# Column tiles for a tail and for routing logits, first-round rows by one-hot products, and an earlier read of the spill count, in a hybrid decoder layer

## The chip, the cores and the metric

One core of a Trainium2 chip runs the whole layer. TensorE (PE), VectorE (DVE), ScalarE (ACT), GpSimd (POOL) and SyncE (SP) each work through a queue of their own and wait for each other by semaphores; SP and POOL also start the transfers (DMA). The metric is the device time of one execution in microseconds, as a median of several. All numbers are float32. The profile comes from one profiled execution.

## The reference, cut to what matters

512 tokens of width 1024, with 16 learned meta tokens in front (L = 528 rows), and one layer:

```
n = rms_norm(h)
u = n @ w_in                     # columns: rwkv r,k,v,wd,ad | sb q,k,v | fox q,k,v | fox forget logit (5) | 3 gates
y_a = rwkv7_time_mix(...)        # 6 heads of 64
y_b = stick_breaking_attention   # 5 heads
y_c = forgetting_attention       # 5 heads
h = h + (g0*(y_a@wp_r) + g1*(y_b@wp_s) + g2*(y_c@wp_f)) @ w_out
t = rms_norm(h)
lg = t @ wg + bg                 # 4 groups;  g_idx = argmax
le = t @ we + be                 # 16 experts, 4 in each group
top 2 experts inside the chosen group, softmax over the two, times p_group
y  = sum_e combine[:, e] * ((silu(t @ w_gate[e]) * (t @ w_up[e])) @ w_down[e])   # hidden width 256
return (h + y)[:, 16:]
```

The values of both attentions are 320 columns wide each, and the forget logit adds 5 columns to the second.

## The kernel before, in words

**Projections.** `qkv_products` (line 1508) is a generator of TensorE steps, one product each. It works through 29 groups of 8 chunks: 20 "q" groups (q and k columns, 128 x 264 products), 8 "v" groups (128 rows by 320 or 325 columns), and one "tail" group: rows 512 to 527 of the values. For these 16 rows it makes two products a chunk, one into PSUM partitions 0 to 15 and one into 32 to 47; each is a step, so the tail has 16. The steps are dealt out by `fill_qkv(n)`. A fixed number of steps goes between the small products of the RWKV recurrence (`META_FILL`, `TURN_FILL`, `LEVEL_FILL` and others, lines 61 to 66); what is left (`HEAD_FILL`, line 331) runs before the recurrence. ScalarE copies each group out (`group_out`, from line 714) at fixed places between its own work. In the recurrence TensorE, ScalarE (`Hm` copy) and VectorE (two masked copies, lines 1113 and 1114) take turns at each of 5 levels in each of three head pairs. `fill_out` counts the copied groups; TensorE waits for all 29 in the last level before it fills with gate products (line 1548).

**Output projection and router.** Tokens lie in four tiles of 128. For each tile TensorE makes two half products with `w_out` (`out_half`, line 1818), VectorE adds the residual (line 1243), TensorE transposes the sum (`second_norm_T`, line 1798), ScalarE and VectorE copy the transposed chunks out (`n2T_low`, `n2T_high`), and `router_logits` (line 1809) makes 8 products with the tile's transposed chunk as the stationary operand and the 20 router columns `rw` as the moving one. Tiles 0 to 2 have their logits behind the second half product of the tile after; tile 3 last. ScalarE takes the norm's scale and writes the normalised rows to `n2`; SP stores them to `n2_rows` in HBM.

**Routing.** From the logits VectorE finds group and experts (lines 1263 to 1289), TensorE ranks the tokens of each expert by products with a triangle and ones (1845, 1847), VectorE compares ranks with 0..127 (`hit`, line 1299) and TensorE turns the hits into tables of token ids and weights for 12 rounds (line 1857). Idle products (`unread`, line 1841) stand where TensorE waits. Each round t holds 96 slots of expert MAIN[t] and 32 of a shared one. POOL gathers the rows of rounds 0, 1, 2 from `n2_rows` by these ids (line 617), later ones as their buffers come free.

**Rounds.** In round t TensorE transposes gathered rows (`rows_T`, line 1861), runs gate and up products on four 32-column tiles (line 1878), transposes the hidden rows (1891) and runs the down products (1904). Expert weights lie in five places and are loaded by SP in the order of `PLAN`; one place (number 4) is the memory of `n2`. Results go back by scattering DMA with add; the last three rounds add to rows gathered from the output and scatter plainly (line 625). At the end POOL, like the other engines, reads the number of spilled expert blocks and passes a loop of 10 turns that does nothing if there are none (lines 660 to 662).

Of the kernel before, what the change touches and what calls it, by code (L numbers as in the profile page):

```python
# [14 lines left out]
ALU = mybir.AluOpType  # L15
ACT = mybir.ActivationFunctionType
# [89 lines left out]
def hybrid_layer(nc, x, meta, g1, w_in, mu, w_up, w0, a_up, a0, k_k, k_a, r_k, ln_g, ln_b, f_b, q_g, k_g,  # L106
# [4 lines left out]
    with ExitStack() as ctx:  # L111
# [35 lines left out]
        rw = sb("rw", [P, DC, NG + NE])  # L147
# [6 lines left out]
        stat = sb("stat", [P, 16])  # L154
        f_min = sb("f_min", [P, 4])
# [164 lines left out]
        STEPS = (NF + 1) * DC  # L320
# [50 lines left out]
        def _(sp):  # L371
# [23 lines left out]
            sp.wait_ge(par, 16)  # L395
            swapped = lambda z, i: z.rearrange("(c h p) -> h p c", h=2, p=HD)[1 - i]
# [88 lines left out]
            sp.wait_ge(sem("lg_psum"), 1)  # L485
            expert_in(4)
            expert_out(4)
            sp.wait_ge(sem("xg_in0"), 16)
# [29 lines left out]
        def _(pool):  # L518
# [115 lines left out]
            for t in range(3):  # L634
                rows_in(t, t)
# [18 lines left out]
            pool.wait_ge(sem("sum_in1"), 32)  # L654
            for t in range(N_SUM, NR):
                pool.wait_ge(sem("y_low"), t + 1)
                pool.wait_ge(sem("y_high"), t + 1)
                final_rows(t, t % 3)
            pool.wait_ge(sem("ov_ready"), 1)
            n_ov = pool.value_load(ovi[0:1, 0:1], min_val=0, max_val=NOV)  # L660
# [16 lines left out]
        def _(act):  # L677
# [36 lines left out]
            def group_out():  # L714
# [19 lines left out]
                else:  # L734
                    done(a.activation(V[0:16, i, 0:SW], ps[0:16, b, 0:SW], ACT.Copy))
                    done(a.activation(V[0:16, i, SW:], ps[32:48, b, 0:SW], ACT.Copy))
                    done(a.activation(flog[0:16, i, :], ps[32:48, b, SW:SW + FH], ACT.Copy), "fill_out")
# [178 lines left out]
            for t in range(NT):  # L916
# [13 lines left out]
                done(a.activation(n2[:, t, :], h[:, t, :], ACT.Copy, scale=rs), "n2_ready")  # L930
# [40 lines left out]
        def _(dve):  # L971
# [4 lines left out]
            done(v.memset(eps_c, EPS), "ms_ready")  # L976
            for j in range(SC):
                done(v.memset(U[:, j, 0:1], 0.0))
# [97 lines left out]
            done(tt(rw[:], rw[:], g2c.rearrange("p (c a) -> p c a", a=1).broadcast_to([P, DC, NG + NE]), ALU.mult))  # L1076
# [171 lines left out]
            for t in range(NT):  # L1248
                residual(t, 0)
                if t >= 1:  # L1250
                    high_chunks_T(t - 1)
                residual(t, 1)
# [9 lines left out]
            lg_ps = ps[:, 2, 0:NT * NGE].rearrange("p (t e) -> p t e", t=NT)  # L1262
# [30 lines left out]
            dve.wait_ge(sem("rank_psum"), 1)  # L1293
            rank_ps = ps[:, 3, 0:NT * NE].rearrange("p (a b) -> p a b", a=1).broadcast_to([P, 2, NT * NE])
# [684 lines left out]
```

## Time and profile before

| | |
|---|---|
| median of 3 runs | 828.03 us (826.21 to 828.31) |
| profiled execution: its own time | 827.06 us |
| its span, first to last instruction | 825.3 us |
| mean granted TensorE clock | 0.994 |
| busy: PE, weight loads, DVE, ACT, POOL | 97%, 56%, 35%, 25%, 12% |
| HBM read, written | 100.32 MB, 10.50 MB (134 GB/s over the span) |

The span is told as busy time of each engine, as the chain of work that ended last, and as DMA traffic. A product of float32 appears as two records (two passes). In rows "x16" is a count of instructions; "[0.61 <-DVE ...]" is idle time of the engine before a row and what ended it.

### The profile page before, as it was taken

Reading aid. Unit: us, or ns where it says so; the run is one execution under the profiler, and the core shown is the slowest. Engines: PE = TensorE matmul, PEld = TensorE weight load, DVE = VectorE, ACT = ScalarE, POOL = GpSimd, SP = SyncE. Lnnn points to the kernel's source line nnn. Section 1 sums busy time; section 2 is a strip of 40 time slices with the busy share of each in tenths; the row PEclk is TensorE's granted clock in tenths of the full one; section 3 lists DMA queues with packets and bytes.
Section 4 is the critical chain, followed back from the end, with each engine's and each line's share of the span. In section 5 each row is a group of like instructions: output and inputs, shape, how many; then the busy total and the mean of one; then the engine's idle time right before and its main releaser. Section 6 shows DMA issues by size and latency. Waiting matters only on the chain.

```text
span 825.3 us, 16795 instructions
## 1 busy us (share of the span) xinstructions
PE 800.2 (97%) x7237; PEld 463.8 (56%) x7237; DVE 287.9 (35%) x542; ACT 202.9 (25%) x406; POOL 102.5 (12%) x214
## 2 busy tenths in 40 slices
PE   9999999999999899899999999999999989999995
PEld 8888888877776554455555555444455533333331
DVE  5334930033333245454444333355211423121122
ACT  4324201122253302334432212710112200111100
POOL 8850000000020100131100000000000011211211
PEclk9999999999999999999999999999999999999998
DMA  7412218100000020536111130754630687999962
GB/s 209 116 51 60 95 52 221 36 3 3 4 4 4 3 53 0 128 71 200 51 52 52 51 77 16 240 172 159 256 152 25 253 318 268 373 382 386 389 252 82
DMA packets 76297, 109.80 MB, mean 133 GB/s; under 512 B 17051, under 2 KB 61227, under 8 KB 72128
## 3 DMA queue, kind: packets, MB, share of 16 engines
q1 hardware_dynamic: 71456, 93.22, 33.6%
q0 software_dynamic: 4768, 15.52, 6.4%
q8 instruction: 57, 0.93, 0.5%
q14 instruction: 16, 0.13, 0.0%
HBM read 100.32 MB, written 10.50 MB: 134 GB/s over the span
## 4 chain that ended last, share of the span: by engine, by line
PE 94%; DVE 3%; DMA 1%; issue 1%; SPq 0%; ACT 0%; POOL 0%; POOLq 0%; DVEq 0%; ACTq 0%
PE ps L1548 21%; PE ps L1878 10%; PE ps L1525 9%; PE ps L1443 9%; PE ps L1824 7%; PE ps L1616 7%; PE ps L1785 5%; PE ps L1904 5%; PE ps L1530 5%; PE ps L1721 2%; PE ps L1768 2%; PE ps L1865 2%; PE ps L1427 1%; PE ps L1752 1%; PE ps L1792 1%; PE ps L1756 1%
## 5 line engine op out<-in xcount | busy, mean ns | idle before, releaser
L1548 PE MATMUL ps<-arena 128*128 128x512 f32 x304 | 141.1, 604 | 0.0
L1548 PEld LDWEIGHTS ps<-arena 128*128 128x128 f32 x304 | 54.2, 189 | 58.9 <-issue 58.1
L1878 PE MATMUL ps<-arena 128*32 128x512 f32 x624 | 86.0, 598 | 0.1
L1443 PE MATMUL ps<-arena 128*128 128x264 f32 x320 | 72.8, 386 | 0.0
L1443 PEld LDWEIGHTS ps<-arena 128*128 128x128 f32 x320 | 60.0, 189 | 11.6 <-ACT arena L758 0.7
L1616 PEld LDWEIGHTS ps<-arena 64*64 64x64 f32 x2784 | 51.5, 134 | 21.9 <-issue 16.2
L1616 PE MATMUL ps<-arena 64*64 64x64 f32 x2784 | 56.9, 220 | 4.3 <-DVE arena L1114 2.4
L1525 PE MATMUL ps<-arena,h 128*128 128x264 f32 x256 | 60.5, 389 | 0.0
L1824 PE MATMUL ps<-arena 128*128 128x512 f32 x128 | 56.2, 594 | 0.0
L1525 PEld LDWEIGHTS ps<-arena,h 128*128 128x128 f32 x256 | 47.5, 189 | 8.6
L1785 PE MATMUL ps<-yT_all,arena 128*128 128x512 f32 x112 | 50.1, 599 | 1.0 <-DMA arena<-in_w_p_fox 1.0
L1878 PEld LDWEIGHTS ps<-arena 128*32 128x32 f32 x624 | 22.9, 109 | 45.1 <-issue 45.1
L1332 DVE TENSOR_TENSOR arena<-ps,chan 128x512 f32<-128x512 f32 x24 | 15.6, 686 | 84.5 <-PE ps L1865 84.4
L1904 PE MATMUL ps<-arena 128*32 128x512 f32 x384 | 43.7, 595 | 0.6 <-DVE arena L1349 0.6
L1530 PE MATMUL ps<-arena 128*128 128x320 f32 (+1 forms) x128 | 40.8, 452 | 0.0
L617 POOL DMA_INDIRECT arena<-n_rows,idx x12 | 11.8, 980 | 231.9 <-DVE idx L1316 224.1
L1824 PEld LDWEIGHTS ps<-arena 128*128 128x128 f32 x128 | 23.7, 189 | 28.2 <-issue 28.2
L1206 DVE COPY arena<-ps 128x128 f32<-128x128 f32 (+3 forms) x20 | 9.8, 491 | 81.9 <-PE ps L1756 81.9
L1548 PE MATMUL ps<-arena,yT_all 128*128 128x512 f32 x80 | 38.0, 607 | 0.0
L1878 PE MATMUL ps<-yT_all,arena 128*32 128x512 f32 x144 | 36.4, 602 | 0.0
L1785 PEld LDWEIGHTS ps<-yT_all,arena 128*128 128x128 f32 x112 | 20.7, 190 | 26.8 <-issue 23.9
L947 ACT ACTIVATE arena<-ps 128x256 f32<-128x256 f32 x12 | 4.6, 385 | 96.3 <-PE ps L1878 96.3
(332 smaller groups left out, 983.9 us busy)
## 6 DMA issues: line engine op xcount, KB each, us to landing
arena<-in_moe_w_down SPq DMA_DIRECT2D x32, 512.0 KB, 13.7
arena<-in_moe_w_gate SPq DMA_DIRECT2D x13, 1024.0 KB, 11.2
arena<-in_moe_w_up SPq DMA_DIRECT2D x13, 1024.0 KB, 16.2
arena<-in_w_in SPq DMA_DIRECT2D x19, 512.0 KB, 3.9
arena<-in_w_in SPq DMA_DIRECT2D x5, 1024.0 KB, 6.0
h<-in_x SPq DMA_DIRECT2D x8, 512.0 KB, 5.6
arena<-in_w_out SPq DMA_DIRECT2D x1, 4096.0 KB, 14.9
h<-in_w_in SPq DMA_DIRECT2D x3, 1024.0 KB, 5.2
```

Of the source, the lines that this page charges most:

```text
L1443: ins = mm(ps[:, 2 * (n % 2) + hf, 0:HALF], w[:, c, j * P:(j + 1) * P], nT[:, c, hf * HALF:(hf + 1) * HALF], start=(c == 0), stop=(c == DC ...
L1525: ins = mm(ps[:, b, 0:HALF], w[:, c, (j % 2) * P:(j % 2 + 1) * P], nT[:, c, k * HALF:(k + 1) * HALF], start=(c == 0), stop=(c == DC - 1))
L1530: ins = mm(ps[0:r, b, 0:nw], nT[:, c, k0:k0 + r], w[:, c, 0:nw], start=(c == 0), stop=(c == DC - 1))
L1548: ins = mm(ps[:, gate_bank(n), :], weights_of_gate(n)[:, c, :], nT[:, c, META:L], start=(c == 0), stop=(c == DC - 1))
L1616: return mm(ps[half(q ^ f_out), bank, c * CH:(c + 1) * CH], lhs(r, c), rhs(r, c), start=start, stop=part != "first", skip_group_check=part ...
L1721: ins = mm(psf[:, o + k0:o + k1], QK[q64, cq, qs], QK[q64, ck, k0:k1], start=True, stop=True)
L1768: ins = mm(o, V[:, k, v0:v0 + HD], pT[:, u % 2, j, k, :], start=(k == 0), stop=False, skip_group_check=True)
L1785: ins = mm(ps[:, bank(b), :], wpr[dc % 2][:, 3 * b + c, :], yT[b][:, c, :], start=(c == 0), stop=(b == 0 and c == 2), skip_group_check=(b ...
L1824: ins = mm(ps[:, out_bank(t, k), :], merged[:, c, t * P:(t + 1) * P], wout[:, c, k * 512:(k + 1) * 512], start=(c == 0), stop=(c == DC - 1))
L1865: ins = tr(ps[:, k, c * P:(c + 1) * P], xg[xs_][:, 4 * k + c:D:DC], ident[:])
L1878: ins = mm(ps[rs, bank, :].rearrange("p (h n) -> p h n", h=2), xgT[:, s, c, rs], w1[ws][:, :, c, :], start=(c == 0), stop=(c == DC - 1))
L1904: ins = mm(ps[rs, 4 + k, :], hT[:, s, c, rs], w2[ws][c][:, 512 * k:512 * k + 512], start=(c == 0), stop=(c == 1))
```

## The change

Four edits, with what they need.

- The tail group becomes 8 steps. Each makes four products, of 160, 160, 160 and 165 columns, into PSUM partitions 0, 32, 64 and 96. `STEPS` is 232 instead of 240, so `HEAD_FILL` is 8 less. ScalarE copies it out in four pieces and the forget logits.
- The router weights are padded with zeros to 32 columns. Logits of tiles 0 to 2 come from one function in the middle of the last half product: the weights are stationary, the tokens move, each tile has 32 output partitions. VectorE copies the 96 x 128 result to SBUF, and TensorE transposes it into the place where all logits are read. Tile 3 is done as before with 32 columns.
- Round 0 no longer gathers. VectorE compares ranks for round 0's two experts at once (`hit_ov`), and TensorE multiplies `n2` by these one-hot columns: the result is the transposed rows. `n2` is written in an order in which each chunk of 128 is contiguous. The weights that go over `n2` are loaded only after this.
- POOL reads the spill count before the last three scatters.

```diff
-        rw = sb("rw", [P, DC, NG + NE])
+        rw_pad = sb("rw", [P, DC, 32])
+        rw = rw_pad[:, :, 0:NG + NE]
-        STEPS = (NF + 1) * DC
+        STEPS = NF * DC
...
             par = sem("g1_in")
             sp.wait_ge(par, 16)
+            sp.wait_ge(sem("rw_clear"), 1)
...
             sp.wait_ge(sem("n2_out"), 16 * NT)
             sp.wait_ge(sem("lg_psum"), 1)
+            expert_out(4)
+            sp.wait_ge(sem("xgT_psum"), 2)
             expert_in(4)
-            expert_out(4)
-            sp.wait_ge(sem("xg_in0"), 16)
+            sp.wait_ge(sem("xg_in1"), 16)
             for t in range(NT):
                 sp.dma_start(out[t * P:(t + 1) * P, :], h[:, t, :]).then_inc(sem("sum_set"), 16)
...
             pool.wait_ge(sem("idx_ready"), 1)
-            for t in range(3):
+            for t in (1, 2):
                 rows_in(t, t)
...
             pool.wait_ge(sem("sum_in1"), 32)
+            pool.wait_ge(sem("ov_ready"), 1)
+            n_ov = pool.value_load(ovi[0:1, 0:1], min_val=0, max_val=NOV)
             for t in range(N_SUM, NR):
                 pool.wait_ge(sem("y_low"), t + 1)
                 pool.wait_ge(sem("y_high"), t + 1)
                 final_rows(t, t % 3)
-            pool.wait_ge(sem("ov_ready"), 1)
-            n_ov = pool.value_load(ovi[0:1, 0:1], min_val=0, max_val=NOV)
...
-                    done(a.activation(V[0:16, i, 0:SW], ps[0:16, b, 0:SW], ACT.Copy))
-                    done(a.activation(V[0:16, i, SW:], ps[32:48, b, 0:SW], ACT.Copy))
-                    done(a.activation(flog[0:16, i, :], ps[32:48, b, SW:SW + FH], ACT.Copy), "fill_out")
+                    for n in range(4):
+                        done(a.activation(V[0:16, i, n * SW // 2:(n + 1) * SW // 2], ps[32 * n:32 * n + 16, b, 0:SW // 2], ACT.Copy))
+                    done(a.activation(flog[0:16, i, :], ps[96:112, b, FW // 2:FW // 2 + FH], ACT.Copy), "fill_out")
...
-                done(a.activation(n2[:, t, :], h[:, t, :], ACT.Copy, scale=rs), "n2_ready")
+                done(a.activation(n2[:, t, :].rearrange("p (c q) -> p c q", c=DC), h[:, t, :].rearrange("p (q c) -> p c q", c=DC), ACT.Copy, scale=rs), "n2_ready")
...
             done(v.memset(eps_c, EPS), "ms_ready")
+            done(v.memset(rw_pad[:], 0.0), "rw_clear")
...
                 if t >= 1:
                     high_chunks_T(t - 1)
+                if t == NT - 1:
+                    dve.wait_ge(sem("lgT_psum"), 1)
+                    done(v.tensor_copy(lgT[0:32 * (NT - 1), :], ps[0:32 * (NT - 1), 3, 0:P]), "lgT_ready")
                 residual(t, 1)
...
             dve.wait_ge(sem("rank_psum"), 1)
+            first_rank = R(0)
+            done(stt(first_rank, ps[:, 3, 0:NT * NE].rearrange("p (t e) -> p t e", t=NT), 1.0, asg, ALU.add, ALU.mult))
+            for e, c0, c1 in ((MAIN[0], 0, CAP), (SHARED[0], CAP, P)):
+                done(tt(hit_ov[:, :, c0:c1], first_rank[:, :, e:e + 1].broadcast_to([P, NT, c1 - c0]), rep(iota_f[:, 1:c1 - c0 + 1], c1 - c0), ALU.is_equal), "first_hit")
...
-                            mm(ps[0:r, b, 0:SW], nT[:, c, k0:k0 + r], slot(i - 1)[:, c, 0:SW], start=(c == 0), stop=(c == DC - 1))
-                            yield
-                            ins = mm(ps[32:32 + r, b, 0:RING_W], nT[:, c, k0:k0 + r], w[:, c, 0:RING_W], start=(c == 0), stop=(c == DC - 1))
+                            for n, (cols, wt) in enumerate(((slice(0, SW // 2), slot(i - 1)), (slice(SW // 2, SW), slot(i - 1)),
+                                                            (slice(0, FW // 2), w), (slice(FW // 2, RING_W), w))):
+                                ins = mm(ps[32 * n:32 * n + r, b, 0:cols.stop - cols.start], nT[:, c, k0:k0 + r], wt[:, c, cols],
+                                         start=(c == 0), stop=(c == DC - 1))
...
-            def router_logits(t):
+            def first_logits():
+                pe.wait_ge(sem("n2T_low"), NT - 1)
+                pe.wait_ge(sem("n2T_high"), NT - 1)
+                for c in range(DC):
+                    for t in range(NT - 1):
+                        ins = mm(ps[32 * t:32 * t + 32, 3, 0:P], rw_pad[:, c, :], n2T[:, c, t * P:(t + 1) * P], start=(c == 0), stop=(c == DC - 1))
+                ins.then_inc(sem("lgT_psum"), 1)
+
+            def last_logits():
...
-                    ins = mm(ps[:, 2, t * (NG + NE):(t + 1) * (NG + NE)], n2T[:, c, t * P:(t + 1) * P], rw[:, c, :], start=(c == 0), stop=(c == DC - 1))
+                    ins = mm(ps[:, 2, 32 * t:32 * t + 32], n2T[:, c, t * P:(t + 1) * P], rw_pad[:, c, :], start=(c == 0), stop=(c == DC - 1))
...
+                    if (t, k, c) == (NT - 1, 1, DC // 2):
+                        first_logits()
                     ins = mm(ps[:, out_bank(t, k), :], merged[:, c, t * P:(t + 1) * P], wout[:, c, k * 512:(k + 1) * 512], start=(c == 0), stop=(c == DC - 1))
...
-                if t >= 1:
-                    router_logits(t - 1)
             second_norm_T(NT - 1, 1)
-            router_logits(NT - 1).then_inc(sem("lg_psum"), 1)
+            pe.wait_ge(sem("lgT_ready"), 1)
+            tr(ps[:, 2, 0:32 * (NT - 1)], lgT[0:32 * (NT - 1), :], ident[0:32 * (NT - 1), 0:32 * (NT - 1)])
+            last_logits().then_inc(sem("lg_psum"), 1)
...
-            unread(3)
+            unread(2)
+            pe.wait_ge(sem("n2T_low"), NT)
+            pe.wait_ge(sem("n2T_high"), NT)
+            pe.wait_ge(sem("n2_ready"), NT)
+            pe.wait_ge(sem("first_hit"), 2)
+
+            def first_rows(k):
+                for c in range(4 * k, 4 * k + 4):
+                    for t in range(NT):
+                        ins = mm(ps[:, k, (c % 4) * P:(c % 4 + 1) * P], n2[:, t, c * P:(c + 1) * P], hit_ov[:, t, :], start=(t == 0), stop=(t == NT - 1))
+                ins.then_inc(sem("xgT_psum"), 1)
+            first_rows(0)
             for j in range(2):
...
-            unread(7)
+            first_rows(1)
+            unread(1)
...
-                        ins = tr(ps[:, k, c * P:(c + 1) * P], xg[xs_][:, 4 * k + c:D:DC], ident[:])
+                        ins = tr(ps[:, k, c * P:(c + 1) * P], xg[xs_][:, (4 * k + c) * P:(4 * k + c + 1) * P], ident[:])
...
-            rows_T(0, 0, 0, 16)
```

Left out are the counts of landed gathers, which follow from the gather that is gone, and the two readings of padded logits.

## Rows read from the trace of the kernel before

**Rows 1.** Page, part 4: shares of the chain that ended last, by engine.
```profile
PE 94%; DVE 3%; DMA 1%; issue 1%; SPq 0%; ACT 0%; POOL 0%; POOLq 0%; DVEq 0%; ACTq 0%
```

**Rows 2.** Chain that ended last, 120 to 284 us: start, us, what.
```profile
119.85 39.42 PE ps L1525 x177
...
215.66 2.92 PE ps L1530 x10
...
256.67 1.84 PE ps L1530 x6
...
259.17 1.09 PE ps L1616 x64
...
261.35 1.14 PE ps L1616 x64
...
264.24 1.16 PE ps L1616 x64
...
282.48 1.94 PE ps L1548 x4
```

**Rows 3.** Waits, 100 to 270 us: engine, line, releaser: total us, times, longest.
```profile
DVE arena L1086 <- PE ps L1575: 39.2, 1, 39.2
```

**Rows 4.** Chain that ended last, 600 to 648 us.
```profile
609.66 1.70 PE ps L1815 x16
...
642.48 0.44 PE ps L1806 x4
...
645.94 1.08 PE ps L1815 x8
```

**Rows 5.** Timeline, 642 to 646 us: start, us, engine, line, operation, [idle before].
```profile
642.58 0.69 DVE L1243 TENSOR_TENSOR h<-h,ps 128x512 f32<-128x512 f32 x1 [6.18 <-PE ps L1824]
...
644.46 0.63 PE L1806 MATMUL ps<-ident,h 128*128 128x128 f32 x4
...
645.20 0.69 DVE L1247 COPY arena<-ps 128x512 f32<-128x512 f32 x1 [1.93 <-PE ps L1806]
```

**Rows 6.** Chain that ended last, 653 to 808 us.
```profile
653.70 0.30 DVE arena L1295
...
655.07 0.70 DVE arena L1299
...
657.12 1.96 PE ps L1857 x16
...
661.38 5.97 DMA arena<-n_rows,idx
...
669.11 8.22 PE ps L1878 x60
...
800.55 7.01 PE ps L1878 x64
```

**Rows 7.** Windows: us, busy of PE, PEld, DVE, ACT, POOL, clock, DMA share, GB/s.
```profile
668.00:671.50 3.50, 3.39 (x18) 1.28 (x20) 1.38 (x2) 0.00 (x0) 0.94 (x1) 0.51 1.02 410
```

**Rows 8.** Timeline of ScalarE, 278 to 283 us.
```profile
281.29 0.43 ACT L735 ACTIVATE arena<-ps 16x320 f32<-16x320 f32 x1
...
282.21 0.17 ACT L737 ACTIVATE arena<-ps 16x5 f32<-16x5 f32 x1
```

**Rows 9.** Window of line 1427 (128-column products) alone: us, PE, PEld, clock, DMA.
```profile
12.90:14.80 1.90, 1.90 (x18) 1.90 (x18) 1.00 0.36 61
```

**Rows 10.** DMA issues at 743.4 to 744 us: count, median us to landing.
```profile
arena<-n_rows,idx POOLq DMA_INDIRECT x1, 13.4
```

**Rows 11.** Line 1815 (logits): ns minimum, median, maximum, first and last start.
```profile
L1815 PEld LDWEIGHTS ps<-rw,arena x64: 186/192/192, 609.1 to 646.7; 128*128 128x128 f32 x64
```

**Rows 12.** Lines 660, 661 and 111 in POOL's queue, 810 to 826 us.
```profile
L660 POOLq TENSOR_LOAD <-ovi x1: 509/509/509, 817.1 to 817.1; - x1
L661 POOLq MOVE  x11: 29/29/38, 817.9 to 822.0; - x11
...
L111 POOLq DRAIN  x1: 2688/2688/2688, 822.4 to 822.4; - x1
```

More of the change, by code:

```diff
@@ L154, in hybrid_layer @@
         stat = sb("stat", [P, 16])
+        lgT = sb("lgT", [P, P])
         f_min = sb("f_min", [P, 4])
@@ L1075, in _ @@
             dve.wait_ge(sem("g1_in"), PARAMS_B)
-            done(tt(rw[:], rw[:], g2c.rearrange("p (c a) -> p c a", a=1).broadcast_to([P, DC, NG + NE]), ALU.mult))
+            done(tt(rw, rw, g2c.rearrange("p (c a) -> p c a", a=1).broadcast_to([P, DC, NG + NE]), ALU.mult))
             dve.wait_ge(sem("consts_ready"), 2)
@@ L1261, in _ @@
             dve.wait_ge(sem("lg_psum"), 1)
-            lg_ps = ps[:, 2, 0:NT * NGE].rearrange("p (t e) -> p t e", t=NT)
+            lg_ps = ps[:, 2, 0:NT * 32].rearrange("p (t e) -> p t e", t=NT)[:, :, 0:NGE]
             done(tt(lgx, lg_ps, row3(stat2[:, 2 * NT:3 * NT], NGE), ALU.mult))
@@ L1807, in second_norm_T @@
                 ins.then_inc(sem("n2T_psum"), 1)
-            def router_logits(t):
+            def first_logits():
[6 more added lines that the diff above has]
+            def last_logits():
+                t = NT - 1
                 for c in range(DC):
@@ L1913, in down_ov @@
                     ins.then_inc(sem("down_low" if k == 0 else "down_psum"), 1)
-            pe.wait_ge(sem("n2T_low"), NT)
-            pe.wait_ge(sem("n2T_high"), NT)
-            rows_T(0, 0, 0, 16)
             for t in range(NR + 1):
@@ L1930, in _ @@
                     pe.wait_ge(sem("xgT_ready"), 2 * t + 2)
-                    rows_T(t + 1, (t + 1) % 2, (t + 1) % 3, 16 * ((t + 1) // 3 + 1))
+                    rows_T(t + 1, (t + 1) % 2, (t + 1) % 3, 16 * ((t + 1) // 3 + ((t + 1) % 3 > 0)))
                 if t >= 1:
@@ L1947, in _ @@
                     ins.then_inc(sem("slots_psum"), 1)
-                    rows_T(t, 0, 0, k * 16 + 16 * (NR // 3 + 1))
+                    rows_T(t, 0, 0, k * 16 + 16 * (NR // 3))
                     gate_up_ov(t, k * 32 + 32 * (SLOT0_LOADS + 1))
```

## The prediction

> **What bounds the kernel now.** First the shares of the chain that ended last [rows 1]: 94% of the span is TensorE. So a microsecond counts only where TensorE issues it or waits for it. I then went to the places where the change touches TensorE's order: the projection stage, the output projection with the router, the start of the expert stage, and the end. In the projection stage TensorE runs products of the q, k, v columns one after the other [rows 2], while VectorE has nothing to do for 39.2 us [rows 3]: there each product saved is time saved. From 215 us on the same products are fillers between the small products of the recurrence [rows 2]. At 256 us a filler of three v products lasts 1.84 us; when the fillers become the short tail products, TensorE stands until VectorE is ready: the recurrence's products end at 261.35 + 1.14 = 262.49 and go on at 264.24, 1.75 us later. There a filler under 1.75 us is free. The router [rows 4, 5] is a chain on TensorE with one hop over VectorE; the routing [rows 6] is a chain over both; then comes 5.97 us of a row gather for which TensorE waits, and a first round (8.22 us) that is 1.2 us longer than a later one (7.01 us), since the granted clock is 0.51 over its first 3.5 us [rows 7]: 1.2 instead of 2.4 GHz, after TensorE had run out of work during that gather.
>
> **Tail values on four column tiles.** The last group was 16 filler steps (two products of 320 and 325 columns for each of 8 chunks); now it is 8 steps of four products of 160 to 165 columns. The fillers in the recurrence keep their number of steps, so the 8 steps come out of the projection stage before them, and every group slides 8 places later.
> - Projection stage: 8 products of 2 passes fewer, 39.42 / 177 = 0.223 us a pass [rows 2]: -3.6. VectorE's wait of 39.2 us [rows 3] says that what follows is ready earlier; I take all of it.
> - Filler places that turn from v to q: a v pass costs (2.92 - 1.84) / 4 = 0.27, a q pass 0.22. Two steps (4 passes) lie where nothing else is waited for: -0.2. The others lie in fillers that VectorE's 1.75 us bounds.
> - The filler before the third head pair: now five v steps like the one at 215.66 (2.92), before 259.17 - 256.67 = 2.50: +0.4.
> - Two fillers of three tail steps become three v steps: 1.84 for 1.75, together +0.2. Three tail steps of four tiles each are under 1.75 us: nothing, VectorE's two masked copies hide them. If that cover were gone they'd cost 3 x 0.27 + 0.22 = 1.0.
> - ScalarE takes the group out in four copies instead of two, then the 5-column one. 320 columns are 0.43 us, 5 are 0.17 [rows 8]; by the line between them 160 are 0.30. Four are 4 x 0.33 = 1.3 with the gaps, two were 2 x 0.46 = 0.9: +0.4. TensorE's next product starts at 282.48 [rows 2], 0.1 us behind the 5-column copy's end: it waited for it, so the 0.4 is on the path.
> Sum -2.8 (bounds: -1 if the sliding opens a wait in each level, -3.8 if the added ones hide).
>
> **Three tiles' logits side by side.** Removed: two calls of 1.70 us [rows 4], and the third, 1.70 us. Added in the middle of the last output product: 8 chunks of three 32-column tiles, 128 moving columns each. No row has this shape; the nearest is the warm-up product of 128 columns, 1.90 / 18 = 0.106 us a pass [rows 9], so 16 passes are 1.7 us if the tiles run beside each other; above, 5.1 us if they don't. I take 1.7: the expert products with their four 32-column tiles do 64 records in 7.01 us [rows 6], that is four tiles in the time of one. To this two changes of tile shape: a filler of 6 passes takes 1.84 where 6 x 0.27 = 1.62, so 0.2 each, 0.4. The last output product has the third call behind it, so up to its end (642.48 before) the path is 3.4 shorter and 2.1 longer: -1.3. Its waits (the transposed rows of tile 2) were asked for an output product earlier; the copy of the logits by VectorE lies before the last residual sum, which waits for TensorE anyway: nothing.
> Behind 642.48: the residual sum ends at 642.58 + 0.69 = 643.27, and the last four transposes, at 644.46 before because the third call stood ahead of them, can start at 643.3 [rows 5]: 1.1 earlier. The copy to n2T (645.20) and the last four logits products (645.94, 1.08) follow them. The transpose of the 96 logits rows and the first four products (0.1 + 0.9) fit into the 0.7 + 0.7 that this hop takes. -1.1. Sum -2.4 (bounds +1 to -3).
>
> **First rows by one-hot products.** Before: routing, gather, transposes, round one. Now, on the times of the trace before: the rank products end at 653.6 [rows 6].
> - VectorE gets three operations ahead of its chain: 64, 384 and 128 elements a partition. 128 are 0.30, 512 are 0.70, so 0.3 + 0.57 + 0.3 = 1.2. The slot values, for which the slot products waited until 657.1, come at 658.3.
> - TensorE: two idle products (4 passes of 512 columns, 7.01 / 16 = 0.44 each) to 655.3; VectorE's hits are there at 653.7 + 1.2 = 654.9. Then 16 products, 32 passes of 128 columns at 0.106: 3.4, to 658.7. The slot products (16 passes, 1.7) to 660.4, for which nothing is waited now. Second 16 products, to 663.8. One idle product, to 664.7. The scaled rows: VectorE has the first half after the slot tables and a copy of the ranks (about 663.4), the second 0.7 (its price for 512 elements) behind 663.8, and round one needs it half a round later. Round one starts at 664.8 instead of 669.1: -4.3.
> - The gather's 5.97 us and the stretch without work in it are gone, and I expect the clock to stay: round one at 7.01 instead of 8.22, -1.2. If it fell all the same, this is the loss.
> - Next late: rows of round two. POOL now asks for them first. The gather was issued 2.3 us behind the slot products (661.38 for 659.08), now at 662.95, landing at 668.9 if it takes 5.97; wanted at 664.8 + 7.0 = 671.8. Cover 2.9 us. Behind it in the queues: two more gathers, one expert's gate and up weights (2 MB), held back until the second 16 products have read n2 (their place), and the four stores of h, which wait for round two's rows. Those weights are wanted three rounds later.
> - ScalarE now writes n2 with strided reads of h; no row has such a read. The last residual sum ends at 643.3 [rows 5] and n2 is wanted at 655.3: 12 us for one tile's norm and copy. Nothing.
> Sum -5.5 (bounds: -1 if the gather takes the 13.4 us of the longest one [rows 10] and the clock falls, -6).
>
> A rule speaks against this part. The row: in the warm-up each pass has its weight load and the pace is still 0.106 us [rows 9]; the logits products have loads of 192 ns [rows 11] at 1.70 / 16 = 0.106 a pass [rows 4]. So loads hide behind the pass before, with other weights too. The Trainium skill (TensorE: Matmul & The Clock Gate, The mechanism) says that a weight load runs beside matmuls in flight only when its row group differs; here all have all rows. By it the sum would be that of the third rival; by the rows it is as above.
>
> **Spill count.** The read on POOL (817.1) and what belongs to it stood between the last scatter and the loop (817.9); then comes the loop, and a drain of 2.69 us from 822.4 [rows 12]. Now it is ahead of the three last scatters; what it reads was written in round one, and the third scatter waits for VectorE's last rows, so a first one that goes 0.8 later holds nobody up. -0.8, if the drain has a length of its own; 0 if it waits for the scatter.
>
> **Sum.** -2.8 - 2.4 - 5.5 - 0.8 = -11.5, on the profiled execution's 827.06 (span 825.3): 815.6. That execution is 0.97 under the median of the runs (828.03), from which it would be 816.5. I say 816.0. The memory set of the router weights stands on VectorE ahead of its wait for the first loads, and SP's wait for it behind SP's own for a gain vector: nothing.
>
> **Rivals.**
> - Late rows. If the gather for round two takes 13.4 us as the longest of the trace did [rows 10] instead of 5.97, it eats the cover and 4.5 us more: 820.5. For it: the held weights and the stores come in the same stretch. Against: it is issued ahead of both.
> - Tiles don't run beside each other: logits +3.4; the tail's 64 passes of 0.135 (0.27 x 160/320) are 8.6 us where some 3.6 are covered, +5: 824.4. Against: the expert rows [rows 6].
> - Slower: loads exposed. If each pass of the new short products carries its load of 0.192 [rows 11] alone, 64 passes of the one-hot products cost 12.3 and 16 of the logits 3.1: 831.4. It decides from (828 - 816) / 80 = 0.15 us exposed a pass. Against: [rows 9, 11] as read above.
>
> **How the numbers follow.** Forecast 0.83, with its own range 813.5 to 818.5 (the small bounds; the clock's 1.2; the drain's 0.8). Late rows 0.10, tiles 0.04, exposed loads 0.03. The range reaches from 813.5 to the late rows, 820.5. All but the last are faster by far more than 0.3% (2.5 us), about what a measurement of this kernel can tell from no change: faster 0.96, same 0.01, slower 0.03.
>
> **What would show it.** In the profile after: the run of q products before the recurrence ends 3.6 us earlier; the tail's rows have four tiles at 0.14 us a pass; ScalarE's copies end 0.4 us later against the small products; three logits tiles in one 1.7 us block; last transposes right behind the residual sum; 64 records of one-hot products at 0.106 us; no clock below 1.00 between 640 and 810; round one about 7.0 us; POOL's drain at 821.6 less the shift of all before. Wrong would be: a gap on TensorE before round two's transposes, a one-hot pass over 0.15 us, or a gap at the new order's first recurrence level.

## The result, and the profile after

The changed kernel takes 814.4 us (median of 4 runs, 813.7 to 815.4) against 827.7 before (4 runs, 826.2 to 828.3): a ratio of 0.985, 95% interval 0.983 to 0.987. Forecast were 816.0 us and a range of 813.5 to 820.5. The profiled execution took 814.37 us (span 812.6), 12.7 less than that of before.

The shares of the chain that ended last, by engine (the row that answers to [rows 1]): TensorE has gone from 94% to 96%, and the DMA's 1% is gone.
```profile
PE 96%; DVE 2%; issue 0%; ACT 0%; POOL 0%; POOLq 0%; DVEq 0%; ACTq 0%
```
The projection stage and the end of the recurrence, from the chain (start us, us, what), against [rows 2]: the last run of q products is 36.97 us. The 39.42 of [rows 2] is only the part of that run from 119.85 on; the whole run before is the first row below, so 16 passes and 3.56 us are gone. The other rows are those of the kernel after. In the levels of the tail, TensorE waits for VectorE's two masked copies (lines 1118 and 1119), so the four-tile steps cost nothing. ScalarE's four copies of 0.30 and the one of 0.18 end at 278.82, and TensorE starts behind them.
```profile
118.73 40.53 PE ps L1525 x182
```
```profile
119.39 36.97 PE ps L1538 x166
...
268.88 0.75 DVE arena L1118
...
269.66 0.74 DVE arena L1119
...
277.32 0.30 ACT arena L740
...
278.64 0.18 ACT arena L741
...
278.86 2.84 PE ps L1561 x6
```
Two rows of TensorE's timeline show a tail filler of three steps, 24 records in 1.03 us, and the idle time behind it. The filler of two steps ahead of it, 16 records, takes 0.75. So a step of two passes takes 0.28 us, and a pass over four tiles 0.14, as forecast.
```profile
273.56 1.03 PE L1535 MATMUL ps<-arena 128*16 128x160 f32 x24
275.42 1.16 PE L1629 MATMUL ps<-arena 64*64 64x64 f32 x64 [0.83 <-DVE arena L1119]
```
At the first level of the new order, where the prediction called a gap a sign of being wrong, TensorE idles 0.24 us for the masked copies (at 179.1). The stretch up to there takes no longer than before (23.01 us from the first recurrence product, 23.05 before).

The router, against [rows 4, 5]: 48 records of three tiles in 1.88, so 16 passes at 0.118; the last transposes follow the residual sum; the transpose of the logits (L1861) and the last products come at once.
```profile
632.12 1.88 PE ps L1828 x48
...
637.74 0.70 DVE h L1248
...
638.48 0.66 PE ps L1819 x4
639.14 0.08 PE ps L1861
639.23 1.86 PE ps L1838 x16
```
The start of the expert stage, against [rows 6]: rank products, one idle pair, one-hot products, slot products, one-hot products, idle product, round one. No DMA is in the chain, and the next rows' transposes (666.27) follow round one without a gap.
```profile
646.38 0.44 PE ps L1870 x2
...
647.66 1.81 PE ps L1866 x4
649.48 3.57 PE ps L1885 x32
653.05 1.71 PE ps L1894 x16
654.75 3.65 PE ps L1885 x32
658.41 0.86 PE ps L1866 x2
659.27 7.00 PE ps L1916 x64
666.27 0.60 PE ps L1903 x4
...
676.08 1.02 PE ps L1903 x8
```
The first 3.5 us of round one as a window of that line (PE, PEld, clock, DMA share, GB/s), against [rows 7]: the granted clock is 1.00 (2.4 GHz).
```profile
659.20:662.70 3.50, 3.50 (x36) 1.08 (x40) 1.00 0.93 339
```
At the end POOL's last scatter starts at 805.54, and in POOL's queue the drain of 2.6 us still follows at its own length, now from 809.8 (against [rows 12]). The chain of before shows the read of the count (L660) ahead of the start of the last scatter, not behind it as the prediction has it: from the end of VectorE's last rows to that start it takes 1.15 us before and 0.85 after, so 0.3 of the gain lies there and the rest behind. The chains of before, then after:
```profile
817.10 0.51 POOLq L660
817.61 0.67 POOL out L625
```
```profile
805.54 0.97 POOL out L629
```
The drain after:
```profile
L111 POOLq DRAIN  x1: 2607/2607/2607, 809.8 to 809.8; - x1
```
The clock did fall somewhere else. In the kernel after, TensorE waits 2.13 us (328.24 to 330.37) for VectorE's scan and sum behind five small transposes; then come the chain rows below, with 8 products of 5.33 us; the window behind them has a granted clock of 0.50 (1.2 GHz). The kernel before has the same wait, 3.6 us later and 2.50 us long, and had no fall there in its profiled execution.
```profile
330.37 0.73 PE ps L1734 x4
331.10 5.33 PE ps L1561 x8
```
```profile
331.60:335.00 3.40, 3.40 (x6) 1.34 (x5) 0.84 (x2) 2.33 (x4) 1.75 (x2) 0.50 1.15 289
```

### The profile page after: what moved, and what is told of

It is laid out like the page before. It is cut to its first block, busy times and chain, and to the rows that moved or that the text cites. A ratio compares the mean times of both kernels' runs of the same rounds, so it can differ in the third digit from the quotient of the medians.

```text
span 812.6 us, 16955 instructions
## 1 busy us (share of the span) xinstructions
PE 793.5 (98%) x7312; PEld 464.0 (57%) x7312; DVE 289.6 (36%) x547; ACT 207.1 (25%) x408; POOL 101.3 (12%) x213
## 4 chain that ended last, share of the span: by engine, by line
PE 96%; DVE 2%; issue 0%; ACT 0%; POOL 0%; POOLq 0%; DVEq 0%; ACTq 0%
PE ps L1561 22%; PE ps L1916 10%; PE ps L1455 9%; PE ps L1538 9%; PE ps L1849 7%; PE ps L1629 7%; PE ps L1798 6%; PE ps L1942 5%; PE ps L1543 5%; PE ps L1734 2%; PE ps L1781 2%; PE ps L1439 1%; PE ps L1765 1%; PE ps L1903 1%; PE ps L1805 1%; PE ps L1885 1%
## 5 line engine op out<-in xcount | busy, mean ns | idle before, releaser
L1455 PEld LDWEIGHTS ps<-arena 128*128 128x128 f32 x320 | 60.1, 189 | 11.5 <-ACT arena L762 0.7
```

The costliest lines, as they stand in the source:

```text
L1455: ins = mm(ps[:, 2 * (n % 2) + hf, 0:HALF], w[:, c, j * P:(j + 1) * P], nT[:, c, hf * HALF:(hf + 1) * HALF], start=(c == 0), stop=(c == DC ...
```

## The experiments

All times below are medians with the ratio to the kernel before on the same chip, 95% interval in brackets. A "fall" is a stretch in which the granted clock is 0.50. Each trace is divided at the same records of TensorE's order. "Head" is first transposes to first recurrence product; "scores" is from the gates' small transposes (328 us after, 331 before) to the first transposes of probabilities; "router" is from the first out product to the rank products; "start" is rank products to round one; "round 1" goes to the first down products, "rounds" to the last ones, "end" to the end of the span. The stretches between these are left out. Differences of record starts, us:

```
kernel              head   scores  router  start  round 1  rounds   end    falls of the clock at (us)
before            149.54    7.40    71.28  16.80   19.10   123.79  13.30   668
e4 spill          149.52    9.05    71.90  15.98   17.95   123.79  12.43   334, 648
e5 busy gather    149.66   10.46    71.28  17.64   17.95   123.79  13.31   333 (twice as long), 661
e11 before+fill8  149.51    7.40    71.28  16.49   17.96   123.82  13.32   658
e2 router         149.51    8.72    69.29  17.33   20.07   123.82  13.34   334, 644, 665 (twice as long)
e3 one-hot        149.51    9.00    71.90  12.72   17.83   123.21  13.27   333, 647
e1 tail           146.06    9.09    71.28  15.92   17.95   123.79  13.31   333, 657
after             145.94    8.73    68.69  12.82   17.83   123.20  12.37   332
e12 after again   146.34    7.03    68.70  12.82   17.83   123.20  12.43   none
e7 tight          145.94    8.72    68.69  11.78   17.84   123.20  12.57   332
e8 fill of 16     145.94    8.60    68.69  12.82   17.83   123.20  12.61   none
e9 fill of 8      146.18    7.03    68.70  12.82   17.83   123.20  12.39   none
e10 fill8+tight   145.95    7.03    68.69  13.41   17.83   123.20  12.39   648
e6 strided        145.94    8.64    69.29  20.73   17.96   123.82  12.64   331, 641, 662
```

**Each part alone (e1 to e4).** Each is the kernel before with the hunks of one part of the diff and nothing else.

> The kernel before with the tail values' change alone (four 32-column tiles, the head and the fillers between its levels). Theory: as in my sum, the head is 3.6 us shorter and some of it goes back in the turns, so the time falls by 2.4 to 3.6 us (ratio 0.9957 to 0.9971) and round one still has its stretch at half clock at 668 us. Rival: the fall of the granted clock to 0.5 that the changed kernel shows at 331.6 us (against a steady clock in the same place of the kernel before) belongs to this part, because it moves the recurrence against the idle place behind it; then this kernel shows a fall there too, and its gain is only 1 to 2 us (ratio 0.9976 to 0.9988).

e1: 823.1 us, ratio 0.995 [0.994, 0.997], 4.1 us less and a little more than expected. Head -3.5. The fall that was expected in round one isn't there (it came at 657 us). The fall at 333 us is there, but it is no mark of this part: e2, e3 and e4 have it too. The rival falls.

> The kernel before with the routing logits' change alone (three tiles side by side, the fourth later). Theory: the traces of before and after differ by 1.5 us from the output projection to the end of its last out product and by 1.1 us from there to the rank products, so the time falls by 2.4 to 2.7 us (ratio 0.9967 to 0.9971). Rival: a part of those differences comes from the output projection's weights, whose transfer was waited on for about 1.1 us in the trace of before and not in that of after, and goes with any shorter head; then this kernel alone gives the same 2.4 to 2.7 at these two places, but its head stretch up to the output projection is unchanged, wait included. If the third tile's sums were late (my rival of the prediction), the gain would be under 1 us.

e2: 825.7 us, ratio 0.998 [0.997, 1.000], 1.5 us less. Router -2.0, since in this execution the clock fell at 644 us and the ten idle passes ahead of the rank products took 6.07 us and became what the rank products wait for; in the traces without that fall it is -2.6. The expected ratios, 0.9967 to 0.9971, only touch the end of the interval (0.9970 to 0.9996). The wait for the projection weights (about 1.1 us from 520 to 580 us before) was shorter here too, by 0.7.

> The kernel before with the one-hot rows of round one alone (and the normalised rows in a column order without stride). Theory: round one starts 4.0 us earlier, the clock doesn't fall in it (1.2 us), and the later rounds' transposes read without a stride, 0.06 us for each of the rounds (0.6 us): together 5.8 us (ratio 0.9930). Rival A: the clock falls anyway at some other time, then 4.6 us (ratio 0.9944). Rival B: the weight loads of the 64 one-hot products are exposed (0.19 us each beside 0.11), then round one starts about when it did and the gain is under 1 us.

e3: 822.8 us, ratio 0.996 [0.994, 0.997], as rival A has it. Start -4.1 against the trace of before, rounds -0.6, and no fall in round one, but one at 647 us and a mean granted clock over the runs of 0.9925, no better than the 0.9922 of the kernel before on the same chip. The start with a gather varies with the gather: it takes 5.97 us in before, 6.18 in e2, 5.24 in e4 and 5.65 in e11. The starts of e4 and e11 are 15.98 and 16.49 instead of 16.80, and against them the one-hot rows gain 3.3 and 3.8 us. So part of the 4.1 hangs on the execution that it is read from.

> The kernel before with the spill count read ahead of the last scatters alone. Theory: 0.8 to 0.9 us off the end of the program, nothing elsewhere (ratio 0.9989). Rival: the read is not what the end waits for, no change (ratio 1.000).

e4: 825.7 us, ratio 0.999 [0.997, 1.000]. The time alone can't tell the two theories apart; the trace can: the end is 0.87 shorter. What else differs from before are the falls of the clock and the shorter gather.

**The wait for the gather (e5).**
```
-            unread(7)
+            unread(9)
```


> The kernel before, with two more of the unread products (0.86 us each) in the wait for the gathered rows of round one, so that TensorE idles about 0.6 us there instead of 2.3. Nothing else is changed and nothing waits for them. Theory: the stretch at half clock in round one (668.06 to 671.47 us) follows from that idle wait; with the wait filled the clock stays full, gate and up products take 7.0 us instead of 8.2, and the time falls by 1.2 us (ratio 0.9985). Rival: the fall comes whatever the engine did in the wait, no change (within 0.2 us).

e5: 828.3 us, ratio 1.000 [0.998, 1.002]: no gain. The timeline of TensorE's idle products (start, us), and behind it a window from 660 to 664 us (the engines as in the page's part 1, then clock, DMA share and GB/s):
```profile
660.81 9.56 PE L1841 MATMUL ps<-reset,tri_lt 128*128 128x512 f32 x18
```
```profile
660.00:664.00 4.00, 4.00 (x12) 2.30 (x12) 2.00 (x11) 0.00 (x0) 0.69 (x1) 0.58 1.00 411
```
The clock fell earlier, right behind the waits of 0.92 and 0.86 us for the ranks and the slot values. It was full again in round one (17.95 instead of 19.10), but the slow filling pushed round one back (start 17.64 instead of 16.80). So filling the last of three waits gained nothing in the median. That it moved the fall isn't shown: e1, e4 and e11 leave the wait unfilled, and they too have their fall ahead of round one and 17.95 to 17.96 in it. The single executions say more than the median: five of the twelve took 824.4 to 827.0 us at mean clocks of 0.994 to 0.997, the other seven 828.1 to 829.7 at 0.990 to 0.994, and the trace is one of the latter. The kernel before had 825.1 to 831.0 at 0.990 to 0.995 on this chip.

**The column order of the normalised rows (e6).** The kernel after, with n2 in its natural order; everything that reads it takes every eighth word.
```
-  mm(ps[...], n2[:, t, c * P:(c + 1) * P], hit_ov[:, t, :], ...)
+  mm(ps[...], n2[:, t, c:D:DC], hit_ov[:, t, :], ...)
```


> The kernel after, with the normalised rows kept in their natural order again, so that the one-hot products and the transposes of all rounds read them with a stride of 8 words (only the copy that makes them is without a stride). Theory: the transposes of a round take 1.08 us instead of 1.02, so the rounds lose 0.6 us, and the one-hot products' loads of strided columns are slower too: 64 products at 0.13 instead of 0.11 would add 1 us; together 0.6 to 1.8 us slower (ratio 1.0007 to 1.0022). Rival: stride costs TensorE nothing and the 0.6 us has another source; no change.

e6: 823.6 us, ratio 0.995 [0.993, 0.997]: by the two ratios 8 to 9 us slower than the kernel after; both theories were far too low. Chain of e6, then the one-hot line (L1885) of e6 and of after, nanoseconds minimum, median, maximum:
```profile
650.05 7.54 PE ps L1885 x32
657.58 1.71 PE ps L1894 x16
659.29 7.70 PE ps L1885 x32
```
```profile
L1885 PEld LDWEIGHTS ps<-arena x64: 313/336/338, 649.6 to 666.5; 128*128 128x128 f32 x64
```
```profile
L1885 PEld LDWEIGHTS ps<-arena x64: 187/192/193, 649.0 to 658.0; 128*128 128x128 f32 x64
```
A strided weight load takes 336 ns instead of 192, and a pass 7.54 / 32 = 0.236 us instead of 0.112: 64 passes cost 8.0 us more. In the table start is 7.9 higher. The weight loads set this pace, not the products: they are busy for all of the 7.50 us from 650.0 to 657.5, and the second group, with the granted clock at 0.50 for 3.4 of its 7.7 us, takes only 0.16 us more than the first. The transposes of the later rounds (L1903), after and then e6: 141 and 193 ns a load; the rounds lose the 0.6 us that e3 and after gain.
```profile
L1903 PEld LDWEIGHTS ps<-ident,arena x88: 138/141/146, 666.2 to 784.5; 128*128 128x128 f32 x88
```
```profile
L1903 PEld LDWEIGHTS ps<-ident,arena x88: 186/193/208, 674.8 to 793.8; 128*128 128x128 f32 x88
```

**Idle products left out (e7).** The kernel after with one idle product fewer ahead of the one-hot products and none ahead of round one (0.86 us each).
```
-            unread(2)
+            unread(1)
...
             first_rows(1)
-            unread(1)
```


> The kernel after, with unread products taken out in two places: one of the two (0.86 us) ahead of the one-hot products, which then start when the hits are there, and the one between the one-hot products and round one. Theory: the first gives 0.5 us (the hits are there at 648.92, the products start at 649.48), the second 0.4 to 0.86 (the rows' copies end at 657.87, round one starts at 659.27), so 0.9 to 1.4 us faster (ratio 0.9983 to 0.9989). Rival: the shorter filling leaves an idle stretch after which the granted clock falls in round one, which costs 1.2 us and gives the gain back; no change or slower.

e7: 813.9 us, ratio 0.983 [0.980, 0.986]. Start is 11.78 instead of 12.82, as the theory says. Only 0.25 of it comes from the first place, where VectorE's hits are then waited for 0.44 us. Whether the whole time is better than that of the kernel after wasn't measured on this chip; e10 below tells more.

**Filling the wait at 328 us (e8, e9, e11), and the changed kernel again (e12).**
```
             ins.then_inc(sem("fcum_psum"), 1)
+            for _ in range(16):      # e8; 8 in e9, e10 and e11
+                mm(ps[:, 6, 0:P], ident[:], ident[:], start=True, stop=True)
```


> The kernel after, with 16 unread products of 128 columns (0.107 us each, 1.7 us together) in the wait of 2.1 us behind the transposes of the cumulated gates at 328 us. Theory: the stretch at half clock at 331.6 us (3.4 us long, eight products took 5.33 instead of 3.63 us) follows from that wait; with it filled the clock stays full and the time falls by 1.7 us (ratio 0.9979). Rival: the fall has no link to the wait, or it comes only in some executions; then no change in the time, or the fall moves to another place.

e8: 815.3 us, ratio 0.986 [0.983, 0.988]. The fall is gone, the gain isn't there: each product is two passes, which I had forgotten, so the filling takes twice what I wrote and ends 1.5 us after the wait that it should bridge. Chain of e8:
```profile
328.14 3.77 PE ps L1755 x32
331.91 0.66 PE ps L1734 x4
332.57 3.63 PE ps L1561 x8
```


> The kernel after, with 8 unread products in the wait behind the transposes of the cumulated gates. Sixteen of them took 3.77 us for a wait of 2.13, so eight should take 1.89 us and end inside it. Theory: the granted clock then stays at full speed behind the wait, as it did with sixteen (eight products of 512 columns 3.63 us instead of 5.33), and nothing is pushed out: the next transposes of scores follow the cumulated gates' by 7.4 us instead of 8.7, and the time falls by 1.3 to 1.7 us against the kernel after (ratio to it 0.9979 to 0.9984). Rival: less filling than sixteen isn't enough, or the fall moves on to the waits at 645 to 649 us; then the time is that of the kernel after.

e9: 814.0 us, ratio 0.984 [0.982, 0.985]. The filling ends inside the wait and the scores take 7.03, better than the 7.4 expected, but the time is that of the kernel after (e12).

> The changed kernel itself, so that the three edits of it have a time on the same chip. Theory: 814 to 815 us, mean granted clock 0.994 to 0.995, one fall at 331 us in the trace. The falls in round one's preparation (641 to 672 us) that every trace with a wait for gathered rows shows are absent, since TensorE has no idle time of over 1 us there. Rival: they come here too in some executions, and the profiled one before was a favourable one.

e12: 813.7 us, ratio 0.984 [0.983, 0.986]: no difference from e9. Here the kernel after itself had no fall in its trace (span 810.2), with nothing in the wait, and mean granted clocks of 0.996 to 0.998 in its runs. So the fall expected at 331 us didn't come, and the clock was higher than expected. Chain of e12:
```profile
329.59 0.73 PE ps L1734 x4
330.32 3.63 PE ps L1561 x8
```
So the same kernel pays 8.73 in one execution and 7.03 in another for this stretch: 1.7 us for a fall that comes or doesn't. Nothing in this trace speaks for the rival of e12, falls in the preparation of round one.

> The kernel before, with the same eight unread products in the same wait. Theory: the kernel before pays for a fall of the clock at that wait too, in most of its executions though not in the profiled one, so it gains 1.0 to 1.7 us (ratio 0.9979 to 0.9988), and its mean granted clock goes up from 0.992 to 0.994. Rival: the fall at that place belongs to the changed kernel; no change here.

e11: 824.9 us, ratio 0.9975 [0.996, 0.999], mean granted clock 0.994 instead of 0.992. As expected, though a little more. That the kernel before pays for this place in most executions, its profiled one being an exception, is argued from this and from e1 to e5: all five traces have this wait unfilled, and all have a fall there.

**Both (e10).**

> The kernel after with both: the eight unread products at 328 us, and the two unread products left out ahead of the one-hot products and ahead of round one. Theory: 1.3 to 1.7 us from the clock and 1.0 us from the filling that is gone (as the trace of that edit alone showed between the rank products and round one), so 2.3 to 2.7 us faster than the kernel after (ratio to it 0.9967 to 0.9972), some 811.5 to 812 us. Rival: with less filling the clock falls in round one in some executions, 1.2 us each, and half of the gain goes back.

e10: 813.5 us, ratio 0.983 [0.981, 0.984], against 813.7 for the kernel after: nothing that can be told apart. The rival happened in the trace: behind the shorter filling the clock fell at 648 us (window 646 to 651, clock 0.66), the first one-hot products took 5.44 us instead of 3.57, and start was 13.41 instead of 12.82. e7 has the same filling there and no fall in its trace.
```profile
647.55 5.44 PE ps L1887 x32
652.99 1.71 PE ps L1896 x16
```
```profile
646.00:651.00 5.00, 4.55 (x20) 3.76 (x20) 4.08 (x13) 0.94 (x1) 0.00 (x0) 0.66 0.99 410
```
No version tried is measurably faster than the changed kernel.

## Why the prediction was right, and where not

The time fell inside its range, and the forecast is 0.2% high. The mechanism is right for the tail, the router, the gather that is gone and the spill count. That the sum came out so close is luck in part: the clock's 1.2 us is no gain that the runs bear out, the tail (0.5), the router (0.2) and the later rounds (0.6) gave more than forecast, and the one-hot rows are priced right only through a change of layout that I had counted at nothing. From one profiled execution to the other:

```
                               forecast  traces  what the runs add
tail: head                      -3.6     -3.6    e1 -3.5
tail: everything behind it      +0.8     -0.7    +0.3 on the mean, see below
router                          -2.4     -2.6    e2 -2.0, with a fall of the clock in it
one-hot: start of round one     -4.3     -4.0    e3 -4.1; -3.3 against the start of e4
one-hot: clock in round one     -1.2     -1.3    e3 -1.3, but paid at 333 and 647 us
one-hot: the other 11 rounds     0       -0.6    e3 -0.6, gone in e6
spill                           -0.8     -0.9    e4 -0.9
clock at 331 us                  0       +1.3    e12: none; e11: before pays it too
projection weights' wait         0       -1.1    58.1 to 59.3 in all traces for that stretch
start of the program             0       +0.7    9.0 to 10.4 us in all traces
sum                            -11.5    -12.7    (the two spans)
```

- **Tail.** The head came out within 0.1. Behind it the forecast was too dear. From the start of the recurrence to 328 us the trace of after is 0.7 shorter than that of before, which is chance as far as the traces tell: over the six traces without this part this stretch takes 171.0 to 171.9 us, and before is the longest of them. The six traces with it, e1 and e9 aside, average 0.3 more than these six. (In e1 and e9 it takes 1.5 more still; in e9 there are pauses of 0.64 and 0.53 us for which the profile names no releaser.) So of the +0.8 the copies' +0.4 is seen row by row (278.86 behind 278.82), and the level fillers came out smaller. Which of them hides was not tried.
- **Router.** -1.5 up to the last out product (forecast -1.3) and -1.1 behind it (-1.1). The block took 1.88 for 1.7 forecast, and the two changes of tile shape, forecast at 0.4, cost next to nothing beside it. Three tiles do run side by side: the second rival falls.
- **Start of round one.** VectorE's hits are ready 2.54 us behind the rank products' start (2.6 forecast), 32 passes take 3.57 and 3.65 (3.4), the idle product and the scaled rows lie where they were put. The gather for round two was issued at 657.08, landed at 662.71 and was wanted at 666.27: a cover of 3.6 us (2.9 forecast), so the late rows of the first rival are nowhere. (The forecast's issue time, 662.95, counts the slot products at the 1.96 us of [rows 6], its own order at 1.7; they took 1.71.)
- **Loads exposed.** The one-hot products all use the full rows, each pass has a load of 192 ns, and a pass takes 112: the loads run beside products and beside each other. e6 shows where loads come into sight: at 336 ns a load a pass takes 236. The Trainium skill (TensorE: Matmul & The Clock Gate, The mechanism) says that a weight load runs beside matmuls in flight only when its row group differs; these rows decide against the "only". The same section also lets a load into the background weight buffer go ahead, which fits them.
- **The step that was missed.** I counted the new column order of n2 as a risk on ScalarE (its copy does take 2.15 us for 1.15 before, hidden as forecast) and at nothing everywhere else. By e6 it carries the part: with n2 in its natural order 7.9 us of start come back, so that round one starts later than before instead of 4 us earlier (start 20.73 in e6, 16.80 before). My 0.106 a pass came from rows with unstrided loads. The price was right only since the change also made these loads unstrided. The same order gives 0.6 us over the later rounds, which I had not looked for. The Trainium skill (SBUF — State Buffer, Door 1: The DMA port swizzle) says that the memory has lines of 16 bytes and that each access that crosses to a new line pays, and puts what can be strided for free at four float32 words. e6's every eighth word lies beyond that, and its 336 ns agree; strides of two or four words were not tried.
- **The clock.** Right in its place and wrong as a gain. I read one execution of before, with one fall, in round one, and took this fall off. The window of [rows 7] is not the first 3.5 us of round one, as I wrote: it starts 1.1 us ahead of the first product, and 2.4 us of it lie in round one. The wait for the gather as the one cause isn't borne out: filled in e5, it gave no gain in the median, and in e4 TensorE idles 1.6 us for the gather without a fall in round one. Nor does every fall follow a pause: those at 648 in e4, 644 in e2, 647 in e3 and 641 in e6 have no pause above 0.5 us since 625 us ahead of them. Over all traces, at 328 us the wait is unfilled in 10 (a fall in 8) and filled in 4 (none). In the preparation and first half of round one, 9 of the 10 traces with gather, strided reads, old router or less filling have a fall; the 4 with all of the change and its filling have none. This grouping was made after the traces were seen, with four of them on one side. By it the change took away a place of falls, and its mean clock is the better one (0.995 and 0.997 in two sets of runs, before 0.992). A part of that lies at the end of the program, where the clock is at 0.50 for the last 7.1 us of the span in before and for 6.5 and 3.7 us in the two traces of after.
- **The sum of the parts.** The four ratios alone add to -1.2%, some 9.8 us; together they are -1.5 and -1.6%. By the stages, without falls and without the transfer's wait, the parts give -3.3, -2.6, -4.7 (with 0.1 for round one) and -0.9: -11.5. (With the start of e4 or e11 in place of that of before, the one-hot rows give up to 0.8 less.) The traces differ by 12.7 and the medians by 13.4 and 13.8, so 1.2 to 2.3 us are left. They fit the higher clock, since the traces of the single parts have two or three falls each and those of the kernel after one and none. One comparison bears on it: with the wait at 328 us filled in both kernels (e11 and e9, one chip) the medians differ by 10.9 us, where unfilled (before and e12, the same chip) they differ by 13.8. So some 3 us of the gain there go with what this filling gives the kernel before and not the kernel after. How much of it is the clock is argued, not shown: the profiled e9 also holds the unexplained pauses named under the tail.

Open stays why the clock falls behind the wait at 328 us in one execution and not in another of the same kernel, and which of the four edits, if any one, makes these falls rarer.

## What to carry to other kernels

Count a changed memory order as a part of its own, and look up for which stride the price of a pass was read: here the layout decided the sign of a part that looks like arithmetic. A fall of the clock seen in one execution is a price with a frequency; before you book it as a gain, look at the same place in several executions, and at whether the fall turns up elsewhere in them. Filling that ends behind the wait costs what it saves: e8's 16 products took away a fall of 1.7 us and put 1.6 us on the path.

## What the runs showed of the hardware that I had not expected

- A 128x128 float32 weight load with every eighth word takes 336 ns (192 unstrided), and the passes go from 112 to 236 ns. The transposes' loads go from 141 to 193 ns, and eight of them from 1.02 to 1.09 us.
- ScalarE's copy of 128x1024 words takes 2.15 us when it reads every eighth word, 1.15 otherwise (after, then e6):
```profile
L934 ACT ACTIVATE arena<-h,stat x4: 2147/2154/2160, 593.9 to 640.1; 128x1024 f32<-128x1024 f32 x4
```
```profile
L934 ACT ACTIVATE arena<-h,stat x4: 1147/1148/1149, 594.0 to 640.2; 128x1024 f32<-128x1024 f32 x4
```
- What a fall of the granted clock costs depends on what TensorE does in it: 1.7 us in the scores (8.73 against 7.03), 1.15 in round one, where 2.4 us of it lay (19.10 against 17.95), 0.6 ahead of the rank products (e3 and e4, 71.90 against 71.28), and 0.16 in e6's second one-hot group (7.70 against 7.54), where the weight loads set the pace.
